# Splitting each weight unit on GpSimd: the high part in four pieces instead of two

## The chip, the core and the metric

The kernel runs on one core of a Trainium2 chip. The metric is the device time of one execution in microseconds (us). All numbers here come from this kernel's timed runs and from one profiled execution. Engine names as in the profile: PE is TensorE (PEld its weight loads), DVE is VectorE, ACT is ScalarE, POOL is GpSimd, SP is SyncE, whose queue issues most loads.

## What is computed

Two layers, one after the other, on 512 positions of width 1024, all in float32. The first is a hybrid block (adaptive norm, a state-space branch and a short convolution branch, gates, an output projection, then a gated feed-forward net); the second a Fourier and windowed-attention block. Cut to the products with weights, which set the length:

```python
mod = silu(c) @ ada_w + ada_b                         # six vectors of 1024
h = rmsnorm(x, mix_pre_g) * (1.0 + sc1) + sh1
proj = h @ w_in                                       # split: z, xbc, dt, sc_b, sc_c, sc_h, gates
y_ssd = ssd_branch(z, xbc, dt_raw, ...) @ w_ssd_out
y_sc = short_conv_branch(sc_b, sc_c, sc_h, sc_conv_w) @ w_sc_out
mix = (g_ssd * y_ssd + g_sc * y_sc) @ w_o
x = x + gt1 * rmsnorm(mix, mix_post_g)
h = rmsnorm(x, ffn_pre_g) * (1.0 + sc2) + sh2
u = causal_dwconv(h @ w_up, ffn_conv_w, ffn_conv_b)
x = x + gt2 * rmsnorm((silu(u_gate) * u_val) @ w_down, ffn_post_g)
# second block
proj = rms_norm(x, norm_w) @ w_in_2                   # u_f, g_f, q, k, v, g_a
out = x + concat([y_f, y_a]) @ w_out_2
```

## The kernel before

The weights come as a stream of 236 units (`UNITS`), each 128 x 1024 float32 (512 KB), that is 8 tiles of 128 x 128. To keep float32 accuracy each operand is used as a high part and a remainder (`h_hi`, `h_lo` for activations, `w_hi`, `w_lo` for weights), and PE makes three products of each tile: hi by hi, lo by hi and hi by lo. A full unit is therefore 24 matmuls of 512 columns.

A unit passes three hands. SP loads it into one of four buffers `raw` (`stream`, L425 to L429, which waits for `split_done` of the unit four before). POOL forms `w_hi` and `w_lo` in one of two slots (`split`, L463 to L474). PE multiplies with it (`unit`, `tiles`, `opening`, `by_class`, `last_by_class`), each after a wait for `split_done`, and raises `units_done` at its end. POOL starts unit u when PE has ended unit u-2 (L483), since that frees the slot; it thus has the time of unit u-1 on PE for the whole split. Nothing of a unit is used before its split is complete: `split_done` is raised by the last `w_lo` instruction alone.

Within a split, POOL issues two `tensor_scalar` instructions (L467), a multiplication by 1.0 twice that rounds `raw` into `w_hi`, each over 512 columns, and then two `tensor_tensor` instructions (L472), `raw` minus `w_hi`, also over 512 columns. The wait on `split_hi` makes each wait for the `w_hi` half that it reads.

The stages in order: the start (adaptive vectors on DVE at L1539, L1551 and L1553, the normalised `h_hi` and `h_lo` at L1560 and L1565, units 0 to 2); four groups of the first block (`group`), in which pieces of the later adaptive vectors are loaded by `load_ada` on the SP queue behind given stream units (`ADA_BEHIND`), accumulated on DVE (L1608) and summed on PE (`ada_sums`, L613); the mix stage (28 units, `MIX_PARTS`, with DVE's `y_lo` L1635 and the gates L1835 to L1841); `w_o`; a norm on DVE, ACT and PE (`norm`, DVE lines L1874, L1885, L1890, L1880) in which the next two units are split; the feed-forward net (`opening`, then `up_round` on DVE), its `w_down`, a second norm; attention; the output.

`opening` interleaves two units tile by tile: the second runs four tiles behind the first, so PE has 12 matmuls left when the first is done and the next unit's split may start.

Of the kernel before, what the change touches and what calls it, by code (L numbers as in the profile page):

```python
# [22 lines left out]
ALU = mybir.AluOpType  # L23
# [6 lines left out]
S = 512  # L30
# [63 lines left out]
def build(nc, arrays):  # L94

    with ExitStack() as ctx:
# [28 lines left out]
        def sem(name):  # L125
            return ctx.enter_context(nc.semaphore(name))
# [11 lines left out]
        raw = keep("raw", [P, 4, UW])  # L138
        w_hi = keep("w_hi", [P, 2, UW], F32R)
# [110 lines left out]
        split_hi = sem("split_hi")  # L250
# [210 lines left out]
        @block.gpsimd  # L461
        def _(pool):
            def split(u, raw_slot, slot, landed):  # L463
                pool.wait_ge(raw_landed[raw_slot], landed)
                for hv in range(2):
                    w = slice(hv * S, (hv + 1) * S)
                    ins = nc.gpsimd.tensor_scalar(w_hi[:, slot, w], raw[:, raw_slot, w], 1.0, 1.0, ALU.mult,  # L467
                                                  ALU.mult).then_inc(split_hi, 1)
                for hv in range(2):
                    w = slice(hv * S, (hv + 1) * S)  # L470
                    pool.wait_ge(split_hi, 2 * u + hv + 1)
                    ins = nc.gpsimd.tensor_tensor(w_lo[:, slot, w], raw[:, raw_slot, w],  # L472
                                                  w_hi[:, slot, w].bitcast(F32), ALU.subtract)
                ins.then_inc(split_done, 1)  # L474

            pool.wait_ge(setup, 1)
            split(0, 0, 0, 16)
            split(1, 1, 1, 16)
            pool.wait_ge(row_stats, 4)
            pool.wait_ge(h_lo_ready, DB)  # L480
            nc.gpsimd.memset(ssd_acc[:], 0.0).then_inc(acc_cleared, 1)
            for u in range(2, UNITS):
                pool.wait_ge(units_done, 1 + u - 1)  # L483
                split(u, u % 4, u % 2, 16 * (u // 4 + 1))
# [1719 lines left out]
```

## Time and profile before

| what | value |
|---|---|
| median of three runs | 1584.72 us (1584.6 to 1586.79) |
| profiled execution's own time | 1586.63 us |
| its span | 1584.8 us |
| PE busy | 1513.6 us, 96% of the span |
| POOL busy | 970.6 us, 61% |
| DVE busy | 789.3 us, 50% |

The span is the time from the first to the last instruction of the profiled execution; its own time is 1.83 us longer. Rows of the profile give the start and length of an instruction in us; a row with x2 stands for two of the same line that follow each other. A bracket behind a row is the idle time of that engine before it and what ended it. L467 is line 467 of the kernel, and so on.

### The profile page before, as it was taken

Reading aid. Unit: us, or ns where it says so; the run is one execution under the profiler, and the core shown is the slowest. Engines: PE = TensorE matmul, PEld = TensorE weight load, DVE = VectorE, ACT = ScalarE, POOL = GpSimd, SP = SyncE. Lnnn points to the kernel's source line nnn. Section 1 sums busy time; section 2 is a strip of 40 time slices with the busy share of each in tenths; the row PEclk is TensorE's granted clock in tenths of the full one; section 3 lists DMA queues with packets and bytes.
Section 4 is the critical chain, followed back from the end, with each engine's and each line's share of the span. In section 5 each row is a group of like instructions: output and inputs, shape, how many; then the busy total and the mean of one; then the engine's idle time right before and its main releaser. Section 6 shows DMA issues by size and latency. Waiting matters only on the chain.

```text
span 1584.8 us, 21453 instructions
## 1 busy us (share of the span) xinstructions
PE 1513.6 (96%) x7486; PEld 1237.3 (78%) x7486; DVE 789.3 (50%) x964; ACT 543.1 (34%) x859; POOL 970.6 (61%) x949
## 2 busy tenths in 40 slices
PE   3898999899899999999799999999899999999998
PEld 3686888788788888888688888888678888888877
DVE  5646566365456656341555555500274473736534
ACT  3362361263046131111532223300243554555432
POOL 1564666565565668777477777776747554555542
PEclk9899999899899999999899999999999999999999
DMA  8253333433433424424132222322252221212131
GB/s 329 82 143 97 116 111 124 142 119 106 146 119 96 155 93 147 134 92 146 54 99 100 93 93 98 101 93 98 88 192 84 67 80 55 78 66 66 66 120 54
DMA packets 65610, 172.08 MB, mean 109 GB/s; under 512 B 5616, under 2 KB 22128, under 8 KB 64912
## 3 DMA queue, kind: packets, MB, share of 16 engines
q1 hardware_dynamic: 45792, 151.47, 28.2%
q10 hardware_dynamic: 19760, 19.86, 4.0%
q8 instruction: 34, 0.56, 0.2%
q14 instruction: 24, 0.20, 0.0%
HBM read 167.05 MB, written 4.26 MB: 108 GB/s over the span
## 4 chain that ended last, share of the span: by engine, by line
PE 87%; DVE 5%; DMA 3%; issue 2%; POOL 1%; ACT 0%; SPq 0%; DVEq 0%; POOLq 0%
PE ps L500 16%; PE ps L503 15%; PE ps L502 15%; PE ps L517 6%; PE ps L519 6%; PE ps L518 6%; PE ps L792 3%; PE ps L794 3%; PE ps L793 3%; DMA ada_raw<-ada 3%; PE ps L940 2%; PE ps L966 1%; PE ps L952 1%; DVE acc L1539 1%; PE ps L688 1%
## 5 line engine op out<-in xcount | busy, mean ns | idle before, releaser
L467 POOL TENSOR_SCALAR w_hi<-raw 128x512 fp32r<-128x512 f32 x472 | 324.6, 706 | 589.3 <-PE ps L503 295.8
L472 POOL TENSOR_TENSOR w_lo<-raw,w_hi 128x512 fp32r<-128x512 f32 x472 | 651.0, 1400 | 0.0
L500 PE MATMUL ps<-h_hi,w_hi 128*128 128x512 f32 x984 | 393.0, 399 | 9.9 <-DVE scp L1723 4.9
L503 PE MATMUL ps<-h_hi,w_lo 128*128 128x512 f32 x984 | 386.4, 393 | 0.0
L502 PE MATMUL ps<-h_lo,w_hi 128*128 128x512 f32 x984 | 386.3, 393 | 0.0
L500 PEld LDWEIGHTS ps<-h_hi,w_hi 128*128 128x128 f32 x984 | 187.1, 190 | 53.0 <-issue 11.8
L503 PEld LDWEIGHTS ps<-h_hi,w_lo 128*128 128x128 f32 x984 | 186.7, 190 | 40.1
L502 PEld LDWEIGHTS ps<-h_lo,w_hi 128*128 128x128 f32 x984 | 187.1, 190 | 39.1 <-issue 1.4
L517 PE MATMUL ps<-h_hi,w_hi 128*128 128x512 f32 x368 | 148.4, 403 | 0.4 <-POOL w_lo L472 0.4
L519 PE MATMUL ps<-h_hi,w_lo 128*128 128x512 f32 x368 | 143.7, 390 | 0.0
L518 PE MATMUL ps<-h_lo,w_hi 128*128 128x512 f32 x368 | 143.4, 390 | 0.0
L1929 DVE SCALAR_TENSOR_TENSOR fcv<-ps,tab,fcv 128x510 f32<-128x510 f32 x88 | 65.7, 747 | 62.5 <-ACT fcv L1332 56.5
L1662 DVE SCALAR_TENSOR_TENSOR cv<-ps,tab,cv 128x509 f32<-128x509 f32 (+2 forms) x72 | 53.8, 749 | 66.6 <-ACT cv L1106 60.3
L1608 DVE SCALAR_TENSOR_TENSOR ada_acc<-ada_raw,small,ada_acc 128x512 f32<-128x512 f32 x56 | 49.9, 920 | 69.0 <-DMA ada_raw<-ada 68.9
L1332 ACT ACTIVATE fcv<-ps,tab 128x512 f32<-128x512 f32 x44 | 34.4, 781 | 138.8 <-PE ps L503 131.2
L1948 DVE RECIPROCAL qrt<-qrt 128x512 f32<-128x512 f32 x24 | 80.2, 3343 | 3.0 <-ACT qrt L1410 3.0
L517 PEld LDWEIGHTS ps<-h_hi,w_hi 128*128 128x128 f32 x368 | 69.1, 188 | 15.2 <-POOL w_lo L472 0.8
L519 PEld LDWEIGHTS ps<-h_hi,w_lo 128*128 128x128 f32 x368 | 69.1, 188 | 14.9
L518 PEld LDWEIGHTS ps<-h_lo,w_hi 128*128 128x128 f32 x368 | 69.2, 188 | 13.0
L1874 DVE RECIPROCAL small<-small 128x1 f32<-128x1 f32 x16 | 2.5, 153 | 142.3 <-ACT small L1273 142.3
L792 PE MATMUL ps<-w_hi,act_hi 128*128 128x512 f32 x176 | 68.5, 389 | 0.0
L793 PE MATMUL ps<-w_lo,act_hi 128*128 128x512 f32 x176 | 68.5, 389 | 0.0
(259 smaller groups left out, 2345.5 us busy)
## 6 DMA issues: line engine op xcount, KB each, us to landing
raw<-stream SPq DMA_DIRECT2D x236, 512.0 KB, 3.2
ada_raw<-ada SPq DMA_DIRECT2D x64, 256.0 KB, 3.9
ada<-ada SPq DMA_DIRECT2D x16, 512.0 KB, 9.2
abc<-acs_dram ACTq DMA_DIRECT2D x16, 512.0 KB, 7.4
x_tok<-x SPq DMA_DIRECT2D x1, 2048.0 KB, 8.2
xr<-x_classes ACTq DMA_DIRECT2D x1, 2048.0 KB, 10.7
x_dram<-xr ACTq DMA_DIRECT2D x1, 2048.0 KB, 10.9
x_res<-x_dram ACTq DMA_DIRECT2D x2, 1024.0 KB, 7.6
```

The source lines that it names most:

```text
L467: ins = nc.gpsimd.tensor_scalar(w_hi[:, slot, w], raw[:, raw_slot, w], 1.0, 1.0, ALU.mult, ALU.mult).then_inc(split_hi, 1)
L472: ins = nc.gpsimd.tensor_tensor(w_lo[:, slot, w], raw[:, raw_slot, w], w_hi[:, slot, w].bitcast(F32), ALU.subtract)
L500: nc.tensor.matmul(ps[:, bank], w_hi[:, slot, w], x_hi[:, k0 + k], start=start and k == 0, stop=False)
L502: nc.tensor.matmul(ps[:, bank], w_hi[:, slot, w], x_lo[:, k0 + k], start=False, stop=False)
L503: mm = nc.tensor.matmul(ps[:, bank], w_lo[:, slot, w], x_hi[:, k0 + k], start=False, stop=stop and k == tiles - 1)
L517: nc.tensor.matmul(ps[:, bank], w_hi[:, slot, w], x_hi[:, k], start=start and m == 0, stop=False)
L518: nc.tensor.matmul(ps[:, bank], w_hi[:, slot, w], x_lo[:, k], start=False, stop=False)
L519: mm = nc.tensor.matmul(ps[:, bank], w_lo[:, slot, w], x_hi[:, k], start=False, stop=signal is not None and m == len(of) - 1)
L792: nc.tensor.matmul(out, x_hi[:, q], w_hi[:, slot, w], start=first, stop=False)
L793: nc.tensor.matmul(out, x_hi[:, q], w_lo[:, slot, w], start=False, stop=False)
L1929: STT(fcv[:, j, late:S], ps[:, j, 0:S - late], col("ffn_w", 16 * i + 4 * j + k), fcv[:, j, late:S], ALU.mult, ALU.add).then_inc(ffn_taps, 1)
L1948: V.reciprocal(qrt[:, j % 3], qrt[:, j % 3]).then_inc(qk_steps, 1)
```

## The change

The `w_hi` of a unit is formed by four instructions of 256 columns instead of two of 512. `split_hi` therefore rises by four in each unit, and the waits of the two `w_lo` halves count accordingly: the first waits for two pieces of its unit, the second for all four. `w_lo` keeps its two halves, and `split_done` is raised as before.

```diff
                 pool.wait_ge(raw_landed[raw_slot], landed)
+                for q in range(4):
+                    w = slice(q * S // 2, (q + 1) * S // 2)
+                    nc.gpsimd.tensor_scalar(w_hi[:, slot, w], raw[:, raw_slot, w], 1.0, 1.0, ALU.mult,
+                                            ALU.mult).then_inc(split_hi, 1)
                 for hv in range(2):
                     w = slice(hv * S, (hv + 1) * S)
-                    ins = nc.gpsimd.tensor_scalar(w_hi[:, slot, w], raw[:, raw_slot, w], 1.0, 1.0, ALU.mult,
-                                                  ALU.mult).then_inc(split_hi, 1)
-                for hv in range(2):
-                    w = slice(hv * S, (hv + 1) * S)
-                    pool.wait_ge(split_hi, 2 * u + hv + 1)
+                    pool.wait_ge(split_hi, 4 * u + 2 * hv + 2)
                     ins = nc.gpsimd.tensor_tensor(w_lo[:, slot, w], raw[:, raw_slot, w],
                                                   w_hi[:, slot, w].bitcast(F32), ALU.subtract)
                 ins.then_inc(split_done, 1)
```

## Rows read from the trace of the kernel before

**Rows 1.** The page's head: span, and busy time of each engine.
```profile
span 1584.8 us, 21453 instructions
PE 1513.6 (96%) x7486; PEld 1237.3 (78%) x7486; DVE 789.3 (50%) x964; ACT 543.1 (34%) x859; POOL 970.6 (61%) x949
```

**Rows 2.** The chain that ended last, by engine, in shares of the span.
```profile
PE 87%; DVE 5%; DMA 3%; issue 2%; POOL 1%; ACT 0%; SPq 0%; DVEq 0%; POOLq 0%
```

**Rows 3.** The page's groups, POOL's two (busy us, mean ns, idle before).
```profile
L467 POOL TENSOR_SCALAR w_hi<-raw 128x512 fp32r<-128x512 f32 x472 | 324.6, 706 | 589.3 <-PE ps L503 295.8
L472 POOL TENSOR_TENSOR w_lo<-raw,w_hi 128x512 fp32r<-128x512 f32 x472 | 651.0, 1400 | 0.0
```

**Rows 4.** Groups by shape on POOL, the two sizes of MEMSET.
```profile
L481 POOL MEMSET ssd_acc<- 128x4096 f32 x1 | 3.5, 3525 | 9.2 <-DVE h_lo L1565 9.2
L2198 POOL MEMSET const-float32-0.0<- 128x1 f32 x1 | 0.1, 99 | 0.2 <-issue 0.2
```

**Rows 5.** Timeline of POOL (start, length), an undisturbed split, the next one's start.
```profile
82.49 1.21 POOL L467 TENSOR_SCALAR w_hi<-raw 128x512 fp32r<-128x512 f32 x2 [1.72 <-PE ps L503]
83.66 2.55 POOL L472 TENSOR_TENSOR w_lo<-raw,w_hi 128x512 fp32r<-128x512 f32 x2
87.93 0.62 POOL L467 TENSOR_SCALAR w_hi<-raw 128x512 fp32r<-128x512 f32 x1 [1.72 <-PE ps L503]
```

**Rows 6.** Timeline of POOL, a split in the feed-forward net after a disturbed one.
```profile
837.06 1.21 POOL L467 TENSOR_SCALAR w_hi<-raw 128x512 fp32r<-128x512 f32 x2 [0.87 <-PE ps L503]
```

**Rows 7.** Waits of PE: in total, times, longest (us).
```profile
PE ps L500 <- POOL w_lo L472: 1.2, 3, 0.5
```

**Rows 8.** Timeline of PE, units 2, 115 and 181 starting.
```profile
58.63 0.50 PE L500 MATMUL ps<-h_hi,w_hi 128*128 128x512 f32 x1 [0.42 <-POOL w_lo L472]
793.15 0.50 PE L500 MATMUL ps<-h_hi,w_hi 128*128 128x512 f32 x1 [0.45 <-POOL w_lo L472]
1169.85 0.50 PE L517 MATMUL ps<-h_hi,w_hi 128*128 128x512 f32 x1 [0.41 <-POOL w_lo L472]
```

**Rows 9.** The chain in order of time (start, us), end of the second group.
```profile
259.99 1.83 POOL w_hi L467 x2
...
263.46 1.31 POOL w_lo L472
...
286.53 3.54 PE ps L613 x16
```

**Rows 10.** Timelines of POOL, DVE and PE in the mix stage.
```profile
585.69 1.79 DVE L1635 TENSOR_TENSOR y_lo<-yg,y_hi 128x512 fp32r<-128x512 f32 x1
...
594.87 1.21 POOL L467 TENSOR_SCALAR w_hi<-raw 128x512 fp32r<-128x512 f32 x2 [0.38 <-PE ps L503]
600.39 1.21 POOL L467 TENSOR_SCALAR w_hi<-raw 128x512 fp32r<-128x512 f32 x2 [1.82 <-PE ps L503]
...
622.15 2.36 POOL L467 TENSOR_SCALAR w_hi<-raw 128x512 fp32r<-128x512 f32 x2 [0.29 <-PE ps L503]
627.96 0.50 PE L500 MATMUL ps<-sc_hi,w_hi 128*128 128x512 f32 x1 [0.29 <-POOL w_lo L472]
...
726.69 1.91 POOL L467 TENSOR_SCALAR w_hi<-raw 128x512 fp32r<-128x512 f32 x2 [0.29 <-PE ps L794]
732.36 1.22 POOL L467 TENSOR_SCALAR w_hi<-raw 128x512 fp32r<-128x512 f32 x2 [1.26 <-PE ps L794]
```

**Rows 11.** Timelines of POOL and DVE in the first norm.
```profile
762.94 1.58 POOL L467 TENSOR_SCALAR w_hi<-raw 128x512 fp32r<-128x512 f32 x1
764.50 1.27 POOL L472 TENSOR_TENSOR w_lo<-raw,w_hi 128x512 fp32r<-128x512 f32 x1
765.47 1.38 DVE L1890 TENSOR_TENSOR xr<-xr,br 128x1024 f32<-128x1024 f32 x1
```

**Rows 12.** Timeline of DVE at the start, before the first h_lo.
```profile
40.14 0.89 DVE L1553 SCALAR_TENSOR_TENSOR coef<-mod,tab 128x8 f32<-128x8 f32 x1
41.06 1.45 DVE L1560 TENSOR_SCALAR hf<-xn,coef,mod 128x512 f32<-128x512 f32 x1
```

## The prediction

> **What bounds the kernel now.** I read the page's head first: PE is busy for 1513.6 of 1584.8 us, so nearly everything else is covered by it [rows 1]. The chain that ended last says the same with a finer grain: 87% of it is PE, but 5% is DVE and 1% is POOL, and the change touches POOL [rows 2]. Before its w_hi instructions POOL idles 589.3 us in all, 2.5 us for each of 236 units [rows 3]. So the question is not what POOL does in sum, but at which few places PE or a critical DVE instruction waits for it. For that I went to the timelines.
>
> An undisturbed split shows the rhythm. It starts at 82.49, its w_lo pair starts at 83.66 and ends at 83.66 + 2.55 = 86.21, and the next split starts at 87.93 after 1.72 us idle [rows 5]. The period of 5.44 us is PE's 24 matmuls (0.227 us each); the split takes 3.72 us of it. So an ordinary unit has room: POOL may take 1.72 us more, less what PE needs of lead. That lead I read in the mix stage, where the idle is smaller. Where POOL idled only 0.38 us before its next start, the start after that came 600.39 - 594.87 = 5.52 us later instead of 5.44; where it idled 0.29, 732.36 - 726.69 = 5.67 later [rows 10]. PE thus loses about 0.46 us minus the idle (0.08 and 0.23 here; the estimate is 0.46 and 0.52 by the two). A split with less idle than about 0.46 us behind it holds PE up; with more it costs nothing.
>
> **The change part by part.** Removed: two w_hi instructions of 512 columns in each of 236 units. Added: four of 256. The columns stay the same, so the cost is two more fixed costs per unit. The trace shows no w_hi piece of 256. From above: if a piece cost as much as a half does now (1.17 / 2 = 0.585 us from start to start [rows 5]), a unit would take 1.17 us more; that is the far end. From below: if the whole 0.585 us were in the columns, nothing would be added. Below nothing is excluded for POOL's own work, since no column is saved. Between them the MEMSETs tell: 128x4096 takes 3525 ns and 128x1 takes 99, so a column costs (3525 - 99) / 4095 = 0.837 ns [rows 4]. At that rate 512 columns are 0.43 us, and 0.585 - 0.43 = 0.155 us of a half is fixed. I take this value, an estimate (w_hi reads as well as writes, so its columns may be dearer and its fixed part smaller): a piece is 0.37 us, and a unit gets e = 2 x 0.155 = 0.31 us longer. The small MEMSET's 0.10 us as a fixed part would give 0.20.
>
> The changed counts of split_hi add no wait: the first w_lo needs two pieces and is issued behind four, the second needs the fourth, and the first w_lo lies between.
>
> Where e is hidden: in units with 1.72 us idle, and in the feed-forward net, where the odd units meet DVE and 0.87 us is left [rows 6]; 0.87 - 0.31 = 0.56 is still above 0.46. That is most of 236 units. If this cover were gone (at e above 0.41), each of 22 odd units would lose the excess.
>
> Where it is not:
> - Units 2, 115 and 181. PE waits for these splits by 0.42, 0.45 and 0.41 us [rows 8]; two of them are the unit after an `opening`, where 12 matmuls (2.7 us) cover a split of 3.7. The lateness goes straight to PE: 3 x 0.31 = 0.93 us. Little else of the wait shows up: 1.2 us in three waits in the page of waits [rows 7].
> - The ends of groups 2 to 4. There the chain runs from the split at 259.99 over the stream load that waits for it in SP's queue (the adaptive loads are queued behind it on SP), their landing, and DVE's sums, to PE's L613 at 286.53 [rows 9]. Everything behind that split moves with it: 3 x 0.31 = 0.93 us. What is late next is the same DMA and DVE chain, so nothing of it is given back.
> - The mix stage. DVE instructions with two SBUF inputs and POOL's take turns there: a y_lo of 0.68 us took 1.79 beside a w_lo [rows 10], and a w_hi pair took 2.36 us instead of 1.21. Between 584 and 727 nine splits have 0.60 us idle or less behind them. I went through them one by one with the 0.46 rule. Single ones lose the full 0.31 (three of them: 0.9). In the run of 616 to 634, where PE already waits 0.29 us [rows 10], delays of neighbours cover each other in part: 0.5. Around 640: 0.2. At 584 the first three y_lo now come in between the shorter pieces in one unit instead of two, by some 0.6. Sum 2.2 us.
> - The two norms. DVE is the chain there, and POOL splits two units beside it. DVE alternates an instruction that reads PSUM (1.28 us, L1885) with one that reads two SBUF tiles (L1890, 1.38 us). Before, POOL got one w_hi half through in the gap, and its w_lo (764.50 to 765.77) let L1890 in with almost no wait at 765.47 [rows 11]. After it, three quarters (1.11 us) stand where one half (0.585) did, so w_lo ends 0.52 us later, and the second L1890 waits for it; the first one waits 0.17 less, as a quarter ends sooner. That makes +0.35, and over the second unit +0.35 again: 0.7 us in each norm, 1.4 in all.
> - The start. The coefficient (L1553, 8 columns) took 0.89 us because a w_lo was under way, and the first hf 1.45 for the same reason [rows 12]. With quarters the coefficient slips in 0.8 us earlier, but unit 1's w_lo halves then end 0.8 us later than before and meet the first h_lo. Followed instruction by instruction, h_lo starts 0.34 us later, and the eight that follow are tied to it: +0.34.
>
> Sum: 0.93 + 0.93 + 2.2 + 1.4 + 0.34 = 5.8 us. On the profiled execution's span this is 1584.8 + 5.8 = 1590.6, and 1592.4 for its own time of 1586.63. The median of the runs is 1.9 us below that profiled time, so the forecast is 1584.72 + 5.8 = 1590.5.
>
> POOL's fixed cost is what this rests on, and rows of the MEMSETs put it at 0.155 us. By the Trainium skill (GPSIMD Engine Reference, Performance pitfalls for Q7 kernels) a read command costs about 102 cycles that do not overlap with the one before; at the 1.2 GHz of its Specifications that is an estimate of 0.085 us for each added piece. No row here shows that part by itself. By it e would be 0.17, and the sum about 3.6 us, 1588.3.
>
> **The rivals.**
> - The fixed part is small (e about 0.1, most of the 0.585 us in the columns). For it: MEMSET reads nothing, so its rate says little on a reading instruction. Against it: the rate matches a column per cycle well enough that a rest is left over. Direct places 6 x 0.1 = 0.6, mix 1.0, norms 2 x 0.4, start 0.2: 2.6 us, 1587.3.
> - Not slower: finer pieces let DVE in sooner. It is one mechanism, at the places where DVE is the chain: an instruction with two SBUF inputs waits for at most 0.37 us instead of 0.62. At the start 0.28 us from the last two L1539 and 0.8 from L1553; in the norms 0.17 for each of 8 L1890; up to 0.4 at each of three group ends: 1.1 + 1.4 + 1.2 = 3.7 gained. It decides if POOL's later w_lo do not land on a DVE instruction; against e = 0.31 at six direct places (1.9) and the mix stage (1.5), it ends at 1584.4, no change; with e near 0.1 at 1582.6, faster. Against it: the w_lo halves (1.26 us) are what DVE really waits for, and they stay whole and come later.
> - More than the places above: at e above 0.41 the feed-forward's odd units fall short. At the far end of 1.17 each has 0.87 - 1.17, below 0.46 by 0.76 us: 22 x 0.76 = 17 us, and the places above cost some 15 more. 1615. The MEMSET rate speaks against it; at e = 0.5 it would be 2 us there and 9 elsewhere, 1596.
> - The change does nothing at all to the time, as PE hides it: then 1584.7. Rows 8 speak against it.
>
> **How the numbers follow.** A difference of 0.2% (3.2 us) is about what a measurement of this kernel can tell. Forecast (e 0.2 to 0.4, total 4 to 8 us): 0.60. Small fixed part or nothing: 0.22, within 0.2% nearly always. DVE let in sooner: 0.08, half of it within 0.2%, half faster. More than the forecast: 0.10. So slower 0.72, within 0.2% 0.23, faster 0.05, with a little of the forecast's lower edge counted as within. The range 1586.3 to 1594.5 leaves out the faster half, the nothing case and the far end.
>
> **What would show it.** In the changed trace a lone w_hi piece should take about 0.40 us, with 0.37 from start to start; 0.32 would mean the small fixed part. The undisturbed split should take 4.03 us and leave 1.41 idle. PE's waits at units 2, 115 and 181 should read 0.7 to 0.8. The feed-forward net (24 matmuls per 5.44 us) must not move. The norm's first transposes should come 0.7 us later after its start. If the whole span grows but POOL's idle stays, or if the feed-forward units stretch, the prediction is wrong in its parts; if the mix stage gains nothing, it is too high by 2.

## The result, and the profile after

The change makes the kernel slower, and by twice what was forecast. The changed kernel takes 1598.77 us (median of 4 runs, 1596.37 to 1599.47), the kernel before, run beside it, 1585.76 (4 runs, 1584.6 to 1587.12): ratio 1.0073, 95% interval 1.0061 to 1.0086, that is +11.6 us (9.7 to 13.6) on 1585.76. (The two medians differ by 13.0 us; the ratio on record is a little below theirs. Every gain or loss of timed runs in this text is worked out from the ratio.) The forecast was 1590.5 with a range to 1594.5. The direction was right; the size was not, and the range did not hold the time.

The profiled execution of the changed kernel took 1599.47 us; its span is 12.9 us above that of before. Its head, chain and groups, which answer to [rows 1 to 3]:

```profile
span 1597.7 us, 21925 instructions
PE 1520.1 (95%) x7486; PEld 1237.5 (77%) x7486; DVE 797.8 (50%) x964; ACT 541.0 (34%) x859; POOL 1053.6 (66%) x1421
...
PE 86%; DVE 5%; DMA 3%; POOL 3%; issue 2%; ACT 0%; SPq 0%; DVEq 0%; POOLq 0%
...
L467 POOL TENSOR_SCALAR w_hi<-raw 128x256 fp32r<-128x256 f32 x944 | 412.9, 463 | 520.2 <-PE ps L503 249.3
L472 POOL TENSOR_TENSOR w_lo<-raw,w_hi 128x512 fp32r<-128x512 f32 x472 | 645.3, 1388 | 0.0
```

POOL is busy 88.3 us more in w_hi (412.9 less 324.6) and its idle shrank by 69.1. PE's busy time grew too (by 6.5 us, 1520.1 less 1513.6), with the same 7486 matmuls: more of them ran at half the clock, as shown below, which no step of the prediction had. PE's waits, in total, times and longest, answer to [rows 7]:

```profile
PE ps L500 <- POOL w_lo L472: 5.1, 7, 1.2
```

POOL's timeline has the undisturbed split that answers to [rows 5]:

```profile
82.45 1.52 POOL L467 TENSOR_SCALAR w_hi<-raw 128x256 fp32r<-128x256 f32 x4 [1.43 <-PE ps L503]
83.93 2.54 POOL L472 TENSOR_TENSOR w_lo<-raw,w_hi 128x512 fp32r<-128x512 f32 x2
87.89 0.41 POOL L467 TENSOR_SCALAR w_hi<-raw 128x256 fp32r<-128x256 f32 x1 [1.42 <-PE ps L503]
```

The split takes 83.93 + 2.54 - 82.45 = 4.02 us (forecast 4.03, 3.72 before), the idle behind it is 1.42 (forecast 1.41), a lone piece 0.41 (forecast 0.40). So e = 0.30 us is right, and what is wrong is the list of places where it counts, and that it is the price of an extra pair of pieces beside a busy DVE too. PE now waits 5.1 us in 7 waits for w_lo instead of 1.2 in 3.

To find the places I took, in both traces, the start of each unit's first w_hi on POOL's timeline; the difference is that unit's shift. The stage costs are differences of shifts, and they add up to the 12.9 us. They belong to one profile of each kernel; what the timed runs confirm of them comes with the experiments.

| units | where | forecast | changed kernel |
|---|---|---|---|
| 2, 115, 181 | PE waits for the split directly | 0.93 | 0.91 |
| 113-115, 179-181 | the two norms | 1.4 | 1.63 |
| 112, 178 | `last_by_class` waits for the unit after | 0 | 0.59 |
| 33-37, 53-57, 73-77 | units before the ends of groups 2 to 4 | with the ends | 2.93 |
| 37-38, 57-58, 77-78 | the ends themselves | 0.93 for both | 2.61 |
| 78-80 | first two units behind the last end | 0 | 1.11 |
| 82-112 | mix stage | 2.2 | 3.08 |
| 116-178 | feed-forward net | 0 | 0.64 |
| 24, 44, 64 | a lone unit in each group | 0 | 0.90 |
| 16-17 | end of group 1 | 0 | -1.36 |
| 0 | ahead of the first w_hi piece | 0 | -0.37 |
| 0-2 | the start | 0.34 | 0.29 |
| 3-6 | behind the wait at unit 2 | 0 | -0.25 |
| the rest | attention, output and others | 0 | 0.19 |

One caution about the base. The profile of before landed its last adaptive load of the second group's end in 6.23 us; two experiments below whose code is the same up to unit 82 needed 8.24 and 9.17 there, and stood 0.90 and 0.82 us later than before at unit 82. So about 1 us of the 12.9 is that execution's luck, which fits the 11.6 of the timed runs.

The direct places on PE's timeline after, to be read with [rows 8]. PE's waits at units 2 and 115 grew from 0.42 and 0.45 to 0.75, as forecast. At unit 181 the wait stayed at 0.40: there the work ahead of it on PE came later by as much as the split did. A wait that stays is thus no proof that nothing was lost. Nor does a wait that grew stay lost: of the 0.29 us of unit 2, 0.25 came back by unit 6. Before, PE waited there for DVE's L1591 (it ended at 69.75, PE's L581 began at 69.81); after, DVE came to L1591 sooner (the six L1588 ahead took 2.08 us instead of 4.49) and ended it at 67.73, and L581 followed the matmul ahead of it.

```profile
58.84 0.50 PE L500 MATMUL ps<-h_hi,w_hi 128*128 128x512 f32 x1 [0.75 <-POOL w_lo L472]
803.79 0.50 PE L500 MATMUL ps<-h_hi,w_hi 128*128 128x512 f32 x1 [0.75 <-POOL w_lo L472]
1182.70 0.50 PE L517 MATMUL ps<-h_hi,w_hi 128*128 128x512 f32 x1 [0.40 <-POOL w_lo L472]
```

The first norm, DVE's timeline after. The four L1890 took 1.38, 1.38, 1.36 and 1.37 us before (one is in [rows 11]):

```profile
772.34 1.23 DVE L1890 TENSOR_TENSOR xr<-xr,br 128x1024 f32<-128x1024 f32 x1
775.00 1.89 DVE L1890 TENSOR_TENSOR xr<-xr,br 128x1024 f32<-128x1024 f32 x1
778.31 1.22 DVE L1890 TENSOR_TENSOR xr<-xr,br 128x1024 f32<-128x1024 f32 x1
780.96 1.89 DVE L1890 TENSOR_TENSOR xr<-xr,br 128x1024 f32<-128x1024 f32 x1
```

The first gains 0.15, the second loses 0.51, and so again: 6.23 instead of 5.49, +0.74. The forecast said 0.17 gained, 0.52 lost, 0.7 in sum. This part of the prediction is confirmed down to the instruction.

At unit 24 it is again a DVE instruction that carries the length of a split to PE. DVE's timeline before, then after:

```profile
195.52 1.33 DVE L1635 TENSOR_TENSOR y_lo<-yg,y_hi 128x512 fp32r<-128x512 f32 x2
```

```profile
194.26 1.63 DVE L1635 TENSOR_TENSOR y_lo<-yg,y_hi 128x512 fp32r<-128x512 f32 x2
```

The first y_lo meets POOL's w_lo, which ends 0.3 us later in the longer split, so the pair takes 0.30 us longer, and unit 25's split, released by PE, starts 0.31 us later. The idle behind POOL's split is still 1.77 us there, so it says nothing of this.

The mix stage shows what an extra piece costs when DVE has work. One unit on POOL's timeline after, which answers to the w_hi pair at 622.15 in [rows 10]:

```profile
629.00 3.50 POOL L467 TENSOR_SCALAR w_hi<-raw 128x256 fp32r<-128x256 f32 x4
632.47 3.37 POOL L472 TENSOR_TENSOR w_lo<-raw,w_hi 128x512 fp32r<-128x512 f32 x2
```

The same view in narrower windows, its four pieces one by one:

```profile
629.00 1.09 POOL L467 TENSOR_SCALAR w_hi<-raw 128x256 fp32r<-128x256 f32 x1
630.07 0.83 POOL L467 TENSOR_SCALAR w_hi<-raw 128x256 fp32r<-128x256 f32 x1
630.87 0.83 POOL L467 TENSOR_SCALAR w_hi<-raw 128x256 fp32r<-128x256 f32 x1
631.67 0.83 POOL L467 TENSOR_SCALAR w_hi<-raw 128x256 fp32r<-128x256 f32 x1
```

DVE's timeline beside them:

```profile
629.74 0.89 DVE L1835 TENSOR_TENSOR gts<-gts 128x512 f32<-128x512 f32 x1
630.56 0.88 DVE L1837 TENSOR_TENSOR gts<-gts,ssd_acc 128x512 f32<-128x512 f32 x1
631.48 0.77 DVE L1839 TENSOR_TENSOR mixf<-gts 128x512 f32<-128x512 f32 x1
```

And PE's, at the start of the unit that needs this split:

```profile
635.90 0.50 PE L500 MATMUL ps<-sc_hi,w_hi 128*128 128x512 f32 x1 [1.23 <-POOL w_lo L472]
```

Each of the last three takes 0.83 us where an undisturbed one takes 0.37: 0.46 us of a DVE instruction lies in front of it. (DVE's 0.77 to 0.89 us hold its own wait for POOL.) Two halves gave DVE two turns in the w_hi part (2.36 us instead of 1.21), four pieces give it four (3.50 instead of 1.52). The split is thus 1.14 us longer where two pieces more cost 0.31 by their fixed part, and PE waits 1.23 us instead of 0.29 [rows 10]. The Trainium skill (SBUF — State Buffer, the section on the two separate sides) says that a GpSimd instruction and a VectorE instruction with two SBUF inputs hold the shared port pair for the whole instruction and block the other. The alternation in these rows agrees, with 0.46 us for each turn of 512 columns. In these rows the number of POOL's instructions sets the number of turns.

The units before the ends of the groups show the same on a smaller scale. Unit 35 on POOL's timeline before, then after:

```profile
270.87 1.56 POOL L467 TENSOR_SCALAR w_hi<-raw 128x512 fp32r<-128x512 f32 x2 [1.73 <-PE ps L503]
272.39 3.15 POOL L472 TENSOR_TENSOR w_lo<-raw,w_hi 128x512 fp32r<-128x512 f32 x2
```

```profile
270.27 2.19 POOL L467 TENSOR_SCALAR w_hi<-raw 128x256 fp32r<-128x256 f32 x4 [1.79 <-PE ps L503]
272.43 3.52 POOL L472 TENSOR_TENSOR w_lo<-raw,w_hi 128x512 fp32r<-128x512 f32 x2
```

The split takes 5.68 us instead of 4.67, which is 1.01 longer, and leaves no idle at all behind it (0.77 before).

The collision behind the last group's end, on POOL's timeline after:

```profile
565.95 1.14 POOL L467 TENSOR_SCALAR w_hi<-raw 128x256 fp32r<-128x256 f32 x3
567.06 4.63 POOL L472 TENSOR_TENSOR w_lo<-raw,w_hi 128x512 fp32r<-128x512 f32 x2
```

On DVE's timeline after:

```profile
568.27 2.29 DVE L1825 TENSOR_TENSOR sc_lo<-ysc,sc_hi 128x2048 fp32r<-128x2048 f32 x1 [1.82 <-ACT sc_hi L1230]
```

POOL's timeline before, the same unit:

```profile
561.56 2.56 POOL L472 TENSOR_TENSOR w_lo<-raw,w_hi 128x512 fp32r<-128x512 f32 x2
```

And DVE's before:

```profile
563.08 3.19 DVE L1825 TENSOR_TENSOR sc_lo<-ysc,sc_hi 128x2048 fp32r<-128x2048 f32 x1 [1.39 <-ACT sc_hi L1230]
```

Before, DVE's 2048-column instruction asked at 563.08, while the second w_lo ran, and had to wait (3.19 us). After, it asked at 568.27, 0.04 us ahead of the second w_lo, got its turn (2.29 us), and w_lo waited about 2.1 us: the pair took 4.63 instead of 2.56. An extra 0.3 us of w_hi was enough to change who is first.

Last, TensorE's clock. After the sums at the end of the last group, the changed kernel's profile shows the granted clock at half for a stretch. Busy times and clock of after in stretches of 2 us (columns: stretch, us, busy PE, PEld, DVE, ACT, POOL, granted clock, DMA share, GB/s):

```profile
558.00:560.00 2.00, 2.00 (x10) 1.69 (x10) 1.85 (x2) 0.00 (x0) 2.00 (x2) 0.89 0.00 0
560.00:562.00 2.00, 2.00 (x6) 1.52 (x6) 0.21 (x2) 0.00 (x0) 1.26 (x1) 0.50 0.00 0
```

The same view of before, behind the same sums:

```profile
554.00:556.00 2.00, 2.00 (x13) 1.78 (x13) 1.71 (x2) 0.00 (x0) 2.00 (x2) 1.00 0.00 0
556.00:558.00 2.00, 2.00 (x10) 1.63 (x9) 1.43 (x2) 0.00 (x0) 0.81 (x1) 1.00 0.12 14
```

The granted clock is 0.50 (1.2 GHz) from 560 to 562 and 1.00 (2.4 GHz) at the same place before. In the chain of waits seven matmuls take 0.43 us each instead of 0.23, which with a part of an eighth is 1.5 us. Ahead of it PE did the 16 narrow matmuls of L613 (one column each) after a short wait of 0.35 us; before, the wait was 0.79 us and the clock stayed. So a longer wait is not what decides. The second group's end has five slow matmuls more than before (13 against 8, +1.0 us), the third group's one fewer. Their number there differs without any change too: 9 and 6 at the second group's end in the profiles of `e3_mix` and `e4_norms`, whose code is that of before up to there.

### The profile page after: what moved, and what is told of

It reads as the page before. It is cut to its first block, busy times and chain, and to the rows that moved or that the text cites. A ratio compares the mean times of both kernels' runs of the same rounds, so it can differ in the third digit from the quotient of the medians.

```text
span 1597.7 us, 21925 instructions
## 1 busy us (share of the span) xinstructions
PE 1520.1 (95%) x7486; PEld 1237.5 (77%) x7486; DVE 797.8 (50%) x964; ACT 541.0 (34%) x859; POOL 1053.6 (66%) x1421
## 4 chain that ended last, share of the span: by engine, by line
PE 86%; DVE 5%; DMA 3%; POOL 3%; issue 2%; ACT 0%; SPq 0%; DVEq 0%; POOLq 0%
PE ps L500 16%; PE ps L503 15%; PE ps L502 15%; PE ps L517 6%; PE ps L519 6%; PE ps L518 6%; PE ps L792 3%; PE ps L793 3%; PE ps L794 3%; DMA ada_raw<-ada 2%; PE ps L940 2%; PE ps L966 1%; POOL w_hi L467 1%; PE ps L952 1%; POOL w_lo L472 1%
## 5 line engine op out<-in xcount | busy, mean ns | idle before, releaser
L467 POOL TENSOR_SCALAR w_hi<-raw 128x256 fp32r<-128x256 f32 x944 | 412.9, 463 | 520.2 <-PE ps L503 249.3
L519 PEld LDWEIGHTS ps<-h_hi,w_lo 128*128 128x128 f32 x368 | 69.1, 188 | 14.9
## 6 DMA issues: line engine op xcount, KB each, us to landing
x_dram<-xr ACTq DMA_DIRECT2D x1, 2048.0 KB, 11.1
```

Of the source, the lines that this page charges most:

```text
L519: mm = nc.tensor.matmul(ps[:, bank], w_lo[:, slot, w], x_hi[:, k], start=False, stop=signal is not None and m == len(of) - 1)
```

## The experiments

Each kernel ran on one chip beside the kernel before. Ratios are to that; one us is 0.063%.

**Length or turns.** This kernel keeps the two halves of w_hi and makes every split 0.3 us longer, as the change does, by a MEMSET and not by more pieces that read:

```diff
+                nc.gpsimd.memset(pad[:], 0.0).then_inc(padded, 1)   # pad: 128x320, read by nobody
                 for hv in range(2):                                 # w_lo in two halves, as before
```

> w_hi stays in two halves, but each split gets one GpSimd memset of 128x320 into a buffer that nobody reads, between w_hi and w_lo: about 0.30 us more per unit (0.27 for the columns and a little fixed), as the four pieces add, without any new point at which VectorE and GpSimd take turns on reads. Theory L (the length of the split is what costs, through splits with little idle behind them and through the chains at the ends of groups): 9 to 13 us slower than before, near the changed kernel. Theory P (the finer turns are the main cost, one more VectorE instruction gets in between the pieces of a split): 3 to 6 us slower, and splits in the mix stage stay at most 0.3 us longer than before while those of the changed kernel are up to 1.1 longer.

Each MEMSET also waits for the one before, which is long done. Measured: 1594.11 us (6 runs), ratio 1.0043 (1.0028 to 1.0059), +6.8 us (4.4 to 9.4): between the ranges of the two theories, nearer to P. Its undisturbed split on POOL's timeline (84.89 + 2.54 - 83.41 = 4.02 us) is as long as that of the changed kernel:

```profile
83.41 1.22 POOL L472 TENSOR_SCALAR w_hi<-raw 128x512 fp32r<-128x512 f32 x2 [1.41 <-PE ps L512]
84.56 0.37 POOL L476 MEMSET pad<- 128x320 f32 x1
84.89 2.54 POOL L480 TENSOR_TENSOR w_lo<-raw,w_hi 128x512 fp32r<-128x512 f32 x2
```

Where DVE is idle it loses what the change loses (units 24, 44, 64: 0.3 each; feed-forward net 0.55; behind the last end 1.12). Where DVE is busy it loses little: 0.19 instead of 2.93 in the units before the ends, 0.54 instead of 3.08 in the mix stage. PE waits 2.7 us in 4 for w_lo against 5.1 in 7. So of the 11.6 us some 6.8 are length, and the other 5 come with the pieces themselves, in the stages where DVE takes its turns between them. (The intervals of the two ratios don't overlap, so that the pieces cost more than their length is shown; the 5 is known to 3 us or so.) The MEMSET stands between w_hi and w_lo and leaves DVE a stretch in which POOL reads nothing; whether the same length filled with reading would cost more was not tested. In the dense stage the MEMSET kept its 0.36 to 0.38 us, where a w_hi piece grew from 0.37 to 0.83. The same section of the Trainium skill (SBUF — State Buffer) lets a VectorE instruction with two SBUF inputs contend only with a GpSimd instruction that reads SBUF; a MEMSET reads nothing, and these rows agree.

**The change stage by stage.** Three kernels use four pieces in some units only, and a fourth everywhere else:

```diff
+                n_hi = 4 if 33 <= u <= 37 or 53 <= u <= 57 or 73 <= u <= 79 else 2     # e2_ends
+                n_hi = 4 if 82 <= u <= 107 else 2                                      # e3_mix
+                n_hi = 4 if 112 <= u <= 115 or 178 <= u <= 181 else 2                  # e4_norms
+                n_hi = 2 if 33 <= u <= 37 or 53 <= u <= 57 or 73 <= u <= 107 else 4    # e12_change_but_dense
```

> Four pieces only in the 17 units at the ends of groups 2, 3 and 4 (units 33 to 37, 53 to 57, 73 to 79), two everywhere else. If the loss found there in the trace of the changed kernel (6.7 us between its units 33 and 81, of which 2.6 by one adaptive load that took 8.8 us to land instead of 6.2) belongs to these units: 4 to 7 us slower than before. If it was mostly the luck of one execution's landing times: 1 to 3 us. My recorded price was 0.9 us.

> Four pieces only in the units 82 to 107 of the mix stage and around it. The two traces differ by 3.1 us from unit 82 to unit 108. If the costs are local and add up: 3 us slower than before (2.3 to 3.8). If the phase that the earlier stages bring with them decides: under 1.5 or over 5.

> Four pieces only in units 112 to 115 and 178 to 181, the two norms and the units after the openings. The traces differ by 1.3 and 1.6 us there (0.97 + 0.30 and 1.25 + 0.31): 2.8 us slower than before if local, of which 0.6 are the two splits that PE waits for in the open and the rest VectorE's waits in the norm. By my recorded prices: 1.4 + 0.6 = 2.0.

> The change (four pieces of w_hi), except in the units 33 to 37, 53 to 57 and 73 to 107, which keep two halves: the stages in which POOL has least room beside VectorE. Theory (about 7 to 8 of the change's 12 us are lost in these stages, and the losses of stages add): the shift is 0.9 at the units after 24, 44 and 64, 2.4 from 112 to 116, 0.6 in the feed-forward net and 1.6 from 178 to 182, in all 5 to 6 us, ratio 1.003 to 1.004, and from unit 33 to 38, 53 to 58 and 73 to 112 nothing. Rival (a later start into a dense stage costs as much as longer splits in it): the dense stages lose again with their own splits as before, 9 us or more, ratio 1.006 and above. Rival (losses do not add, later ones swallow earlier ones): below 4 us, ratio 1.002.

| kernel | median us | runs | ratio to before | us |
|---|---|---|---|---|
| e2_ends | 1588.58 | 12 | 1.0010 (0.9999 to 1.0022) | +1.6 |
| e3_mix | 1590.51 | 12 | 1.0015 (1.0005 to 1.0026) | +2.4 |
| e4_norms | 1589.76 | 12 | 1.0019 (1.0008 to 1.0031) | +3.0 |
| e12_change_but_dense | 1593.81 | 5 | 1.0042 (1.0029 to 1.0056) | +6.7 |

The ends alone cannot be told from no change (-0.2 to 3.5 us). Their expectation had two branches, and the time falls in that of the landing luck (1 to 3 us), not in that of 4 to 7. The profile of `e2_ends`, the execution that took 1590.70 us against a median of 1588.58, has 4.0 us in these units: 1.52 in the units before the ends (2.93 in the changed kernel's profile), 1.40 at the ends (2.61) and 1.12 behind the last one (1.11). So the 6.65 us that the changed kernel's profile shows there are not what the change costs at the ends in a usual run. The other three are slower, `e3_mix` and `e4_norms` by about what was expected (3 and 2.8 us). `e12_change_but_dense`, `e2_ends` and `e3_mix` split the changed units among them (units 80 and 81 aside), and 6.7 + 1.6 + 2.4 = 10.7 us against the 11.6 of the whole change: the losses of the stages add, within intervals that leave the sum open by some 3 us. `e12_change_but_dense` by itself (4.6 to 8.9 us) lies between its two rivals, below 4 and 9 or more, and both fall: later losses don't swallow earlier ones, and a later start into a dense stage doesn't cost as much as longer splits in it. Its profile moves by 0.80 us from unit 33 to 38 and by 1.02 from 73 to 112 all the same, where nothing was changed and nothing expected; the first is like `e3_mix` and `e4_norms`, the second has the fall of the clock (1.3 us).

In `e3_mix` the shift grows by 3.08 us over the mix stage, the same as in the changed kernel, with the two steps of about 1 us in the same units. Its POOL timeline at the unit of the rows above:

```profile
623.64 3.51 POOL L470 TENSOR_SCALAR w_hi<-raw 128x256 fp32r<-128x256 f32 x4
```

In `e4_norms` the shift grows by 0.32 and 0.31 us at units 112 and 178, where it does not move at all in `e3_mix`. There `last_by_class` (L834, L857) interleaves two units and waits for the second one's split after three of the first's eight passes, so that split is short of cover like the one behind an `opening`. The prediction had overlooked this place. The norms of `e4_norms` grow by 1.78 and 0.94 us. Against the changed kernel's 0.68 and 0.95 the first is 1.1 too much, and that is the clock again. The chain of waits of `e4_norms` shows six of the slow matmuls in a row, and the first at full clock after them:

```profile
783.93 0.43 PE ps L543
...
786.06 0.43 PE ps L541
786.49 0.33 PE ps L543
786.82 0.23 PE ps L545
```

**The same number of instructions in w_lo instead.** w_hi in its two halves, w_lo in four quarters:

```diff
-                for hv in range(2):
+                for hv in range(4):
-                    w = slice(hv * S, (hv + 1) * S)
+                    w = slice(hv * S // 2, (hv + 1) * S // 2)
```

> As many instructions as the changed kernel has (six), but the quarters are those of w_lo: w_hi two halves, w_lo four of 256. Undisturbed split about 4.03 us as in the change. Theory L alone: about 7 us slower than before, as the run that was only longer. Theory P (turns): 11 to 13 us slower, as the change; a w_lo quarter holds VectorE for 0.65 instead of 1.25 us, which may give 1 to 3 us of that back in the norms and group ends.

Measured: 1603.93 us (5 runs), ratio 1.0099 (1.0084 to 1.0113), +15.7 us (13.3 to 17.9): more than the change, and more than either theory expected (7, or 11 to 13). The shift over the mix stage is 4.9 us, and PE's waits for w_lo are more than the changed kernel's 5.1 in 7:

```profile
PE ps L504 <- POOL w_lo L475: 6.7, 10, 1.3
```

So it isn't anything particular to w_hi: two more instructions in a split cost 0.7% in w_hi and 1.0% in w_lo. Why those in w_lo cost more is not shown. A w_lo in quarters was also no relief for DVE that would show in the time.

**Fewer instructions.** One w_hi instruction of 1024 columns with w_lo in halves, and one of each:

```diff
-                for hv in range(2):                       # w_hi
+                for hv in range(1):                       # e6_one_hi and e7_one_each: all 1024 columns
-                for hv in range(2):                       # w_lo
+                for hv in range(1):                       # e7_one_each alone
```

> The other way: w_hi in one instruction of 1024 columns, w_lo in its two halves, so a split is one fixed cost shorter (3.72 - 0.15 = 3.57 us undisturbed) and has one turn fewer with VectorE. If length and turns both act as in the change, half as large and with the other sign: 3 to 6 us faster than before. If only shortfalls of slack matter (they are few in the kernel before): 1 to 2 us faster. If a VectorE instruction now waits for 1024 columns of w_hi (1.02 us instead of 0.6) on the critical places, the gain is given back: within 1 us.

> One w_hi and one w_lo instruction of 1024 columns: a split of about 3.42 us, two turns instead of four. VectorE instructions with two SBUF inputs may wait up to 2.4 us for a w_lo. Theory L (length, plus turns): 5 to 9 us faster than before. Rival: the longer hold of w_lo delays VectorE where it is the chain (norms, adaptive sums, y_lo): no gain or up to 5 us slower.

Measured: `e6_one_hi` 1579.07 us (6 runs), ratio 0.9945 (0.9930 to 0.9960), -8.7 us (-6.3 to -11.1): faster than both kernels, by more than any branch of its expectation had. `e7_one_each` 1591.35 us (11 runs), ratio 1.0023 (1.0014 to 1.0032), +3.6 us: slower, as its rival had it. An undisturbed split on POOL's timeline of `e6_one_hi`:

```profile
82.31 1.06 POOL L470 TENSOR_SCALAR w_hi<-raw 128x1024 fp32r<-128x1024 f32 x1 [1.75 <-PE ps L507]
83.46 2.55 POOL L475 TENSOR_TENSOR w_lo<-raw,w_hi 128x512 fp32r<-128x512 f32 x2
```

And of `e7_one_each`:

```profile
82.68 1.06 POOL L470 TENSOR_SCALAR w_hi<-raw 128x1024 fp32r<-128x1024 f32 x1 [1.90 <-PE ps L507]
83.82 2.40 POOL L475 TENSOR_TENSOR w_lo<-raw,w_hi 128x1024 fp32r<-128x1024 f32 x1
```

By length alone they hardly differ from before: 3.70 and 3.54 us against 3.72. (The gap of 0.09 us behind a lone w_hi, since w_lo must wait for all of it, eats most of the saving.) So the gain of `e6_one_hi` is hardly length. Its profile can't account for all of it: that execution took 1583.30 us, the longest of the six, and its span is only 3.3 us below that of before. In it the mix stage shrinks by 1.4 us, as one DVE turn less per split would have it; the ends of groups 2 and 3 give 3.4 and 1.9 us, and there the loads also land sooner (4.94 and 7.48 us against 6.23 and 8.03), so how much of that is the turn is argued, not shown. `e7_one_each` shows the other side, the wait of DVE behind a long instruction. In the second norm of `e7_one_each` L1890 (here L1894) took 1.91, 1.88 and 2.99 us beside the undivided w_lo. In `e6_one_hi` three of them took 1.92, 2.02 and 1.91, and the shift grew by 2.3 us there, some 1.5 of it by matmuls at half the clock (8 more than before). DVE's timeline of `e7_one_each`:

```profile
1145.51 1.88 DVE L1894 TENSOR_TENSOR xr<-xr,br 128x1024 f32<-128x1024 f32 x1
1148.82 2.99 DVE L1894 TENSOR_TENSOR xr<-xr,br 128x1024 f32<-128x1024 f32 x1
```

**The best of both.** One w_hi instruction, except in the units at the start and beside the norms:

```diff
+                n_hi = 2 if u <= 2 or 113 <= u <= 116 or 179 <= u <= 182 else 1
```

> w_hi in one instruction of 1024 columns per unit, except in the units 0 to 2, 113 to 116 and 179 to 182, which keep two halves; w_lo in halves everywhere. The one-instruction kernel lost 1.05 us at unit 115 and 3.45 us at unit 181 against its own gains elsewhere, where VectorE's L1890 met a longer POOL instruction. Theory (a split's fixed part counts everywhere, but beside a norm a long w_hi blocks VectorE): these 4.5 us are mostly kept, so the time is 2 to 4.5 us below the one-instruction kernel's ratio of 0.9945: ratio 0.9915 to 0.993, and the shift from unit 112 to 116 and from 178 to 182 is within 0.3 us of zero. Rival (those losses come from the later landing of streams and not from the length of w_hi at the norms): they stay, ratio 0.9945.

Measured: 1576.04 us (5 runs), ratio 0.9933 (0.9919 to 0.9946), -10.6 us. It beats the kernel before; against `e6_one_hi` it is 0.12% ahead (1.9 us), with overlapping intervals, so that part is not shown by the times, and the rival's 0.9945 is within the interval as well. (Elsewhere its code is that of `e6_one_hi`, and its profile gains as much in the mix stage, 1.46 us, and more at the ends of groups 2 and 3, 4.65 and 2.93, which is again how far two profiles of the same code differ there.) The profile is clear at the places: from unit 112 to 116 the shift moves by -0.24 us, from 178 to 182 by +0.22, and on DVE's timeline L1894 in the second norm is back at its old length:

```profile
1131.38 1.38 DVE L1894 TENSOR_TENSOR xr<-xr,br 128x1024 f32<-128x1024 f32 x1
1134.18 1.36 DVE L1894 TENSOR_TENSOR xr<-xr,br 128x1024 f32<-128x1024 f32 x1
```

The measured ratio lies just outside the expected 0.9915 to 0.993. The expectation counted the losses at units 115 and 181 and forgot that the same kernel had gained 1.15 and 1.14 us one unit earlier, so some 2.2 us was all there was to keep (1.05 - 1.15 and 3.45 - 1.14).

**The collision by itself.** The changed kernel, with DVE's L1825 cut into four instructions of 512 columns (and PE's wait for them raised from 2 to 8):

```diff
-                TT(sc_lo[:, 4 * q:4 * q + 4], ysc[:, 4 * q:4 * q + 4], sc_hi[:, 4 * q:4 * q + 4].bitcast(F32),
-                   ALU.subtract).then_inc(sc_lo_ready, 1)
+                for b in range(4 * q, 4 * q + 4):
+                    TT(sc_lo[:, b], ysc[:, b], sc_hi[:, b].bitcast(F32), ALU.subtract).then_inc(sc_lo_ready, 1)
```

> The changed kernel, but VectorE's sc_lo subtraction of 2048 columns (L1825, two of them at the start of the mix stage) is cut into four of 512. In the changed kernel it got its turn 0.04 us ahead of a w_lo, which then took 3.38 us, and PE lost 1.1 us over units 78 to 80. If that is the cause: that loss goes (split of unit 78 at most 5 us instead of 6.11), 1 us faster than the changed kernel, 10 to 12 us slower than before. If it is something else at that place: unchanged there.

Measured: 1595.85 us (6 runs), ratio 1.0047 (1.0031 to 1.0064), +7.5 us where 10 to 12 were expected. From unit 78 to 80 the shift moves by 0.00 instead of 1.11 us, and on POOL's timeline the w_lo pair takes 3.05 us instead of 4.63:

```profile
563.66 3.05 POOL L472 TENSOR_TENSOR w_lo<-raw,w_hi 128x512 fp32r<-128x512 f32 x2
```

The mechanism is confirmed in the profile. The 4 us by which the whole kernel is better than the changed one are more than this 1.1, and the two intervals just overlap; its profile (+8.7) has a further 2.9 us at the end of the third group (-1.95 instead of +0.99), ahead of the place that was cut. The code ahead of L1825 is that of the changed kernel. In the units before the ends it loses nearly as much (2.44 us against 2.93), at the ends themselves -0.31 against 2.61: the first is the change, the second in large part the execution. Whether the timed runs have the rest from there stays open.

## Why the prediction was wrong, point by point

- **The unit cost e.** Right: 0.30 us, from the MEMSET rates [rows 4]. The rival of a small fixed part fell, and with it the estimate of 0.17 from the page's figure (Trainium skill, GPSIMD Engine Reference, Performance pitfalls for Q7 kernels): the measured e is nearly twice that, so the page's figure for a read command does not stand for the whole fixed part here; what else is in it no run shows.
- **Units 2, 115, 181.** Right, 0.91 for 0.93, though 0.25 us of it came back by unit 6.
- **The norms.** Right in mechanism and size (0.74 us in the first, to be compared with 0.7). Missing was `last_by_class` (0.59 us), a direct place of the same kind as those behind an `opening`.
- **"The ends of groups 2 to 4. ... 3 x 0.31 = 0.93 us."** This is the step that failed, with the price below it, "a unit gets e = 2 x 0.155 = 0.31 us longer", which is a price by fixed parts alone. The forecast let one 0.31 us per end run through the DMA chain and put the units ahead of it at nothing. But the three or four units before each end are dense: DVE works beside their splits, and the split of unit 35 grew by 1.01 us, not by 0.31. They shift by 2.93 us in the changed kernel's profile, by 2.44 in that of `e10_sc_cut` (the same code there), and by 0.20 in `e1_longer`, which has the length without the pieces. In the timed runs this term, put at nothing, is the difference between +11.6 us and the +6.8 of `e1_longer`; length alone comes close to the 5.8 of the forecast. Overlooked too was that 0.31 us can turn round who is first at L1825 (1.11 us, shown by the cut). How much the whole row costs in a usual run stays open: 6.65 us in the changed kernel's profile, less 1.36 that it got back at the end of group 1, 4.0 in that of `e2_ends`, and +1.6 (-0.2 to 3.5) in the timed runs of `e2_ends`, which would hold the 0.93 as well. What differs most between these profiles is the landing of the adaptive loads and PE's clock.
- **The mix stage.** Right in place, sized at 2.2 where the profile has 3.08; the timed runs of `e3_mix` (+2.4, 0.8 to 4.1) would allow either. In part that is luck: of the 2.2, 1.6 came from length, and length without pieces cost 0.54 there in `e1_longer`. The 0.46 rule for PE's lead was nearly right; but the prediction priced a split's growth at 0.31 us everywhere, and in a unit with waiting DVE instructions it is 1.14 (3.50 - 2.36). [Rows 10] already showed this price: a w_hi pair of 2.36 us instead of 1.21 is 0.58 us for each piece that DVE lies in front of. Multiplied by two more pieces it would have given the 1.1 us.
- **"Where e is hidden: in units with 1.72 us idle ..."** The second step that failed. `e12_change_but_dense` has the change in the units for which the forecast had 0.93 + 1.4 + 0.34 = 2.67 us and in those at which e was to be hidden, and it is 6.7 us slower (4.6 to 8.9). The profile of the changed kernel shows 2.13 us that the prediction put at nothing: 0.59 at `last_by_class`, 0.90 at a lone unit in each of three groups, 0.64 in the feed-forward net. The lone unit has idle behind its split, but PE waits for DVE's y_lo, which waits for w_lo; the kernel with the MEMSET loses the same there, so it is length. Feed-forward units with 0.57 us idle lost 0.03 to 0.05 each, 0.64 in all: PE's lead is a bit over the 0.46 us that was assumed, or not quite constant. The row:

```profile
847.77 1.51 POOL L467 TENSOR_SCALAR w_hi<-raw 128x256 fp32r<-128x256 f32 x4 [0.58 <-PE ps L503]
```

- **The start.** Right in this profile. The shift at unit 2 is -0.09, but unit 0 stands at -0.37 already, before any w_hi piece has run, and so does DVE's first L1539 of this stretch (32.90 against 33.27). From there to unit 2 it is +0.29, for 0.34. The coefficient took 0.33 us instead of 0.89 and the first h_lo (L1565) 1.75 instead of 0.68, as forecast. `e12_change_but_dense` has +0.28; `e10_sc_cut`, with the same code, -0.12, so the size hangs on how the two engines happen to meet.
- **The rivals.** "DVE let in sooner" did not happen as a gain, though its mechanism is real: it is the 0.15 us of the first L1890 and the 0.56 of the coefficient. The rival with e above 0.41 named the right range (1596 at e = 0.5) for the wrong reason; e was 0.30, and the rest came from turns.

What stays open: why the granted clock falls at one group's end and not in another trace of nearly the same kernel. At the last end it fell in the changed kernel and in six of the ten experiments, the faster `e6_one_hi` among them, and not in the kernel before, `e3_mix`, `e4_norms` (both the same code as before up to there), `e7_one_each` and `e11_one_but_norms`. It fell in all six kernels that make some splits before that end longer than before, and in none of the three whose code is that of before up to there, so the change may well make it likelier; one profile per kernel doesn't show it, and `e6_one_hi` and `e11_one_but_norms`, the same up to there but for units 0 to 2, differ. It is 1.5 us of the 12.9.

## What to carry to other kernels

Count instructions, not columns, when two engines take turns at a port: each further instruction of a fixed amount of work lets the other in once more, and here an added piece cost 0.15 us where the other engine was idle and about 0.6 us where it was waiting. Look for the best piece size from both sides: larger pieces in the stages in which this engine is what is waited for, smaller ones only where the other engine is the chain (here the norms); the mixed version took 10.6 us off the kernel before, to which the finer pieces had added 11.6. And before a price for one unit is multiplied, read the same instruction in the dense stages, since an undisturbed one shows only the lowest price. And a stage's cost read from one profile of each kernel can be 2 to 3 us off where loads land and the clock moves; a timed run with the change in that stage alone is the check.

## What the runs showed of the hardware

- GpSimd's fixed cost per instruction: a `tensor_scalar` takes 0.40 us for 256 columns, 0.62 for 512 and 1.06 for 1024, and in a row 0.37 and 0.585 from start to start. The last two differ by 0.215 us for 256 columns (0.84 ns a column), leaving 0.155 us fixed.
- GpSimd and a DVE instruction with two SBUF inputs alternate one by one when both have work; a DVE turn of 512 columns costs GpSimd 0.46 us (0.83 against 0.37), one of 2048 columns 2.1 (4.63 against 2.56). A MEMSET on GpSimd kept its 0.36 to 0.38 us in the dense stage.
- A difference of 0.04 us in when an instruction asks can decide an exchange that costs 1.1 us (568.27 against 568.31, the start of the second w_lo).
- TensorE's granted clock fell to 0.50 behind the narrow matmuls of L613 in some traces and not in others, for 1.4 to 1.6 us of lost time where it did at the last group's end. This and the landing of the load ahead of it (4.9 to 9.3 us for 256 KB at the end of the second group) make single profiles of this kernel differ by 1 to 3 us at one place where the code is the same.
